# Waiting for all PSUM banks of a dense unit at its head, and for both halves of an expert's up weights at once, in a two-layer flow-matching step

## What the kernel must compute

```python
shift1, scale1, gate1, shift2, scale2, gate2 = adaln(c_vec, w_ada, b_ada)
h = rms_norm(x, norm1) * (1 + scale1) + shift1
conv_in, q_lat, kv_lat, k_rope, gates = split_projection(h @ w_in)
conv_out = conv_module(conv_in, ...)            # GLU, depthwise conv, LayerNorm, swish, @ w_pw2
att = attend(q, k, v) @ w_o                     # 8 heads, latent attention
g_conv, g_att = split(sigmoid(gates))
x = x + gate1 * ((g_conv * conv_out + g_att * att) @ w_out)
h2 = rms_norm(x, norm2) * (1 + scale2) + shift2
# hier_moe: best of 4 groups, best 2 of its 4 experts; 16 experts of width 256
hid = silu(h2 @ w1) * (h2 @ w3) * comb
x = x + gate2 * (hid @ w2)
```

## Time and profile before

| | us |
|---|---|
| three runs | 977.22, 973.48, 974.01 |
| median | 974.01 |
| profiled execution, its own time | 979.21 |
| span of its instructions | 977.4 |
| PE busy with matmuls in the span | 927.7 |
| DVE busy | 726.9 |
| ACT busy | 501.2 |

### The profile page before, as it was taken

One profiled execution on the slowest core, in us unless ns is written; L12 is line 12 of the kernel. 1 busy time (PEld: TensorE's weight loads), 2 busy tenths in 40 slices (PEclk: granted clock), 3 DMA queues, 4 the chain that ended last, 5 costly groups with the idle time before them and its releaser, 6 DMA issues.

```text
span 977.4 us, 15475 instructions
## 1 busy us (share of the span) xinstructions
PE 927.7 (95%) x5998; PEld 770.9 (79%) x5998; DVE 726.9 (74%) x1214; ACT 501.2 (51%) x718; POOL 39.6 (4%) x62
## 2 busy tenths in 40 slices
PE   3999999989999999999999999998899999999997
PEld 2797789767888778887778968996589977888776
DVE  3568799474855689869956697995658568986995
ACT  4243623375422478647754445226663247874772
POOL 1000000032000000000010000001400000000000
PEclk9899999999999799999999999999999999999999
DMA  9953456501655679939939324541123258993971
GB/s 372 369 213 131 168 223 230 201 1 45 231 199 216 254 291 362 361 129 346 385 128 384 113 109 172 232 157 44 44 93 130 81 192 325 361 372 127 326 277 65
DMA packets 29019, 206.75 MB, mean 212 GB/s; under 512 B 3408, under 2 KB 3440, under 8 KB 4240
## 3 DMA queue, kind: packets, MB, share of 16 engines
q1 hardware_dynamic: 28656, 204.81, 55.5%
q0 software_dynamic: 288, 0.92, 0.3%
HBM read 203.98 MB, written 1.74 MB: 210 GB/s over the span
## 4 chain that ended last, share of the span: by engine, by line
PE 80%; DVE 10%; ACT 5%; issue 3%; DMA 1%; DVEq 0%; SPq 0%; ACTq 0%
PE ps L866 57%; PE ps L853 6%; PE ps L877 4%; PE ps L844 2%; PE ps L1331 2%; DVE w_lo L733 2%; PE ps L1154 1%; PE ps L1071 1%; DVE w_lo L728 1%; ACT w_hi L722 1%; DVE x L2359 1%; ACT kT L1611 1%; DMA x<-x 1%; PE ps L1142 1%; PE ps L1426 1%
## 5 line engine op out<-in xcount | busy, mean ns | idle before, releaser
L733 DVE TENSOR_TENSOR w_lo<-ring,w_hi 128x2048 fp32r<-128x2048 f32 (+2 forms) x102 | 225.8, 2222 | 21.6 <-ACT w_hi L1717 20.8
L866 PE MATMUL ps<-h_hi,w_hi 128*128 128x384 f32 x576 | 198.1, 344 | 6.3 <-issue 2.4
L1717 ACT ACTIVATE w_hi<-ring 128x2048 fp32r<-128x2048 f32 x96 | 183.1, 1914 | 20.8 <-PE ps L866 20.8
L866 PE MATMUL ps<-h_hi,w_lo 128*128 128x384 f32 x576 | 193.4, 336 | 0.0
L866 PE MATMUL ps<-h_lo,w_hi 128*128 128x384 f32 x576 | 193.3, 336 | 0.0
L866 PEld LDWEIGHTS ps<-h_hi,w_hi 128*128 128x128 f32 x576 | 108.1, 188 | 20.8 <-issue 13.0
L728 DVE TENSOR_TENSOR w_lo<-ring,w_hi 128x2048 fp32r<-128x2048 f32 x41 | 93.7, 2289 | 33.3 <-ACT w_hi L722 33.3
L866 PEld LDWEIGHTS ps<-h_lo,w_hi 128*128 128x128 f32 x576 | 108.2, 188 | 0.0
L866 PEld LDWEIGHTS ps<-h_hi,w_lo 128*128 128x128 f32 x576 | 108.1, 188 | 0.0
L1961 DVE SCALAR_TENSOR_TENSOR z<-u,par,z 128x399 f32<-128x399 f32 x180 | 104.7, 632 | 1.5
L866 PE MATMUL ps<-w_hi,hg_hi 128*128 128x512 f32 x256 | 103.2, 403 | 0.8 <-DVE hg_lo L733 0.8
(11 more groups left out here) (270 smaller groups left out, 1407.7 us busy)
## 6 DMA issues: line engine op xcount, KB each, us to landing
ring<-wpre SPq DMA_DIRECT2D x96, 1024.0 KB, 6.9
ring<-wmoe SPq DMA_DIRECT2D x96, 1024.0 KB, 6.5
x<-x SPq DMA_DIRECT2D x1, 1536.0 KB, 7.6
x_out<-x SPq DMA_DIRECT2D x4, 384.0 KB, 3.2
par<-par_in POOLq DMA_DIRECT2D x2, 367.5 KB, 7.0
const<-const_in SPq DMA_DIRECT2D x1, 314.0 KB, 3.1
ckv_out<-ckvT POOLq DMA_DIRECT2D x2, 64.0 KB, 5.1
kr_out<-kr POOLq DMA_DIRECT2D x2, 16.0 KB, 5.1
```

Source lines behind the costliest of these rows:

```text
L733: return nc.vector.tensor_tensor(out, whole, leading.bitcast(F32), ALU.subtract)
L866: m = mm(out, a, b, start=(start and i == 0 and j == 0), stop=(stop and i == n - 1 and j == 2))
L1717: af(w_hi[m % MOE_PLACES], slot(moe_slot(l, m)), ACT.Copy).then_inc(split_hi, 1)
```

## The change

It has two parts. First, a new function `begin_all` makes the waits for all banks of a dense unit ahead of its first product: for every bank it looks up the job that had it before, keeps the last of them per evicting engine, and waits for those. GLU units, gate units and `widen` call it at their heads. In `widen` the wait for the convolution's activations (`await_first`) now stands ahead of the bank waits. Second, `up(e, 0)` of experts 1 to 7 waits until unit m + 1, its own second half, is made as well, and `up(e, 1)` no longer waits for weights. Expert 0 keeps its two waits.

```diff
+                def begin_all(name_indices):
+
+                    last = {}
+                    for name, index in name_indices:
+                        j = JOB[(name, index)]
+                        for n, i, b, _ in [e for e in JOBS[:j] if e[2] == JOBS[j][2]][-1:]:
+                            who, k = TAKEN[(n, i)]
+                            last[who] = max(last.get(who, (-1, None)), (k, (n, i)))
+                    for _, e in last.values():
+                        wait_taken(pe, l, *e)
+                    return [ps_of(name, index) for name, index in name_indices]
+
...
                     w = split_unit("glu", c, KD)
-                    for half, name in enumerate(("glu_a", "glu_b")):
-                        out = begin(name, c)
+                    outs = begin_all([("glu_a", c), ("glu_b", c)])
+                    for half, out in enumerate(outs):
                         split_product(out[:, 0:TOK], w(half * P, (half + 1) * P), tokens).then_inc(psum_full, 1)
...
                     w = split_unit("gate", c, KD)
-                    for half in range(2):
-                        out = begin("gate", 2 * c + half)
+                    outs = begin_all([("gate", 2 * c), ("gate", 2 * c + 1)])
+                    for half, out in enumerate(outs):
                         split_product(out[:, 0:TOK], w(half * P, (half + 1) * P), tokens).then_inc(psum_full, 1)
...
                 def widen(name, n, rhs, await_first=None):
                     w = split_unit(name, n, len(rhs))
-                    for c in range(4):
-                        out = begin(name, n * 4 + c)
-                        if c == 0 and await_first is not None:
-                            await_first()
+                    if await_first is not None:
+                        await_first()
+                    outs = begin_all([(name, n * 4 + c) for c in range(4)])
+                    for c, out in enumerate(outs):
                         split_product(out[:, 0:TOK], w(c * P, (c + 1) * P), rhs).then_inc(psum_full, 1)
...
                         at = e // EPG * P
-                        wait_made(pe, mbase, m)
+                        if e == 0:
+                            wait_made(pe, mbase, m)
+                        elif half == 0:
+
+                            wait_made(pe, mbase, m + 1)
                         if e == 0:
```

## The result

The changed kernel takes 1002.72 us, the median of four runs, where the kernel before takes 974.28 beside it (four runs): ratio 1.0284, interval 1.0263 to 1.0304, 28 us slower. The forecast was 19.9 us slower, 993.9, with a range that ended at 999. Run again beside the last experiments, the changed kernel gave 1.0263 (1.0239 to 1.0287), 26.1 us. The direction and the main mechanism were right; 6 to 9 us were missing. The profiled execution took 1003.08, its span is 1001.3 and its mean granted clock 0.971, against 0.985 before.

The account below looks back on a forecast made before the run. PE was taken to bound the kernel, busy 95% of the span. The terms 6.2 + 5.5 + 2 x 2.4 + 3.4 = 19.9 us on the 974.01 median gave 993.9, range 986 to 999.

Parts of the forecast that it names:

- The hold for bank 0 in both layers: Second `w_o` unit: all four products wait for product 0's eviction; idle 7.3 and 8.3 us, costing 6.2 and 5.5.
- 16.5 forecast: The `w_o` part's predicted terms: 6.2 + 5.5 us for the holds and 2 x 2.4 for the clock.
- The free heads: GLU, gate and `w_pw2` units: their bank waits are long met at the head, so cost 0.
- The hold of 2.6 us at expert 1: First round of each layer: up(1, 0) waits for the `w_lo` of unit 3 and starts 2.6 us later.
- cover of 1.6 at down(0): PE already waits 1.59 us for DVE ahead of down(0), time that the delay at expert 1 runs into.
- the experts cost more: Rival: cover at down(0) is lost and the tight expert heads cost 6.8 us, giving 997.3; chance 0.06.
- 6.2 + 5.5 + 3.4: Waits without the clock: `w_o` unit in layer 0, the same in layer 1, and the experts; 15.1 us.
- The loss by the clock behind each `w_o` hold: PE's idle stretch drops the clock to 1.2 GHz; 2.4 us a layer, ends 0 and 3.0.
- saved wait: 36 bank and 28 weight waits leave PE's queue; worth 0 to 3.1 us, taken as 0.
- 2 x 2.4: The clock's term: 2.4 us in each layer for slower matmuls behind the `w_o` unit's idle stretch.
- the experts: Four tight places a layer, at experts 1 and 4, where up(e, 0) waits for its second half: 3.4 us in all.
- Net 0.9: Cost per layer of expert 1's 2.6 us delay in round 0, after 1.76 us of free time at down(0).

Follow-up runs that it names:

- b: The changed kernel with the experts' waits in `up` as before, so only the dense units' part remains: 991.75 us (1.0175).
- c: The kernel before with one wait added, for bank 0 (product 7) at the head of the second `w_o` unit: 993.31 us (1.0184).
- d: The kernel before with `begin_all` in the GLU and gate units alone: 975.93 us (1.0003).
- m: The changed kernel as it is, measured again beside the last experiments: 1000.79 us (1.0263).
- n: The changed kernel with ten thrown-away matmuls filling expert 1's hold in each layer's first round: 995.83 us (1.0204).
- o: The kernel before with the bank 0 wait at the second `w_o` unit's head and expert 1's wait for both halves: 999.98 us (1.0239).
- g: The kernel before, but `up(e, 0)` of experts 2 to 7 waits for both halves: 980.03 us (1.0052).
- h: The kernel before with `turn` 0 moved ahead of the split of unit 5 in ACT's and DVE's written list: 970.39 us (0.9952).
- i: The kernel before with only expert 1 waiting for both halves, its first-round holds filled with ten thrown-away matmuls: 979.23 us (1.0034).
- j: The changed kernel with thrown-away matmuls in both the `w_o` holds and expert 1's first-round holds: 993.26 us (1.0168).
- k: The kernel before, but only expert 4's first product waits for both halves: 975.84 us (1.0009).

## Why the prediction was right and wrong

**Right.** The hold for bank 0 in both layers, its lengths, and that it is the whole of the dense part: 16.5 forecast, 16 to 18 measured (b, c). The free heads (d). The hold of 2.6 us at expert 1 and its cover of 1.6 at down(0), which the list of waits shows used up in the changed kernel and the rival "the experts cost more" denied. The waits of the change all together: 6.2 + 5.5 + 3.4 = 15.1 forecast, +15.2 at full clock for m. The loss by the clock behind each `w_o` hold: 2.4 forecast, 2.4 and 2.6 in the rows; that the middle between two unlike rows was met so closely is in part luck. No saved wait shows, as costed: in d, whose 22 heads make 18 waits fewer, there is nothing to see. The count of 36 saved bank waits was a slip (the written list of jobs gives 17 a layer, 34), and no term hangs on it.

**Wrong: the size of the clock's term.** It was "2 x 2.4", 4.8 us. The low time of m is 32 us above that of before, by the fit 10.4 us; the 25.6 us between the means of m and before split into 15.2 of waits and 10.4 of clock. The step that failed is the one for "the experts", "Net 0.9": I priced the hold of 2.6 us by what it delays and did not ask what it does to the clock, though the part just before had asked it for `w_o`. The row at hand was an idle time of 4.84 us with a fall of the clock; 2.6 us stood between that and none, and it should have had 2.4 us a layer at least as an upper end. With it the high end of the range would have been 999.2 + 4.8 = 1004, and the range would have held. The Trainium skill ("TensorE: Matmul & The Clock Gate", section "HAM oscillation") says that PE is put back to half rate by such a wait and starts its next burst there: the trace agrees for both `w_o` holds, 0.50 in the hold of layer 0 and behind both. The waits in that section of the Trainium skill are of about 3 to 5 us, longer than expert 1's 2.56, for which the runs alone decide: the clock fell there too, in layer 0 before the burst (0.51), in layer 1 only some 1.5 us into it.

**What that leaves.** Behind expert 1's holds the rows show 2.4 us lost in layer 0 (5.24 against 2.86 in n) and 1.3 in layer 1 (837.22 to 841.51, 4.3 us, against 2.99 in n's layer 0 up to the same product), together 3.7. With 5.0 for `w_o` that is 8.7 of the 10.4. Summed over windows of 1 us, the changed kernel's profile has 58 us of low time, 31 of them at the four holds and 27 elsewhere; the profile of before has 29, none of them at these places. So what the changed kernel has more lies at the holds, and 8.7 us over 31 is 0.28 for each microsecond, near the fit's 0.32. The stretches elsewhere, such as the one around window 814 to 815, come no more often with the holds as far as the profiles tell: 21 us in m, 25 in o and 17 in n, 10 to 32 in d, g, h, i, j and k, which have no unfilled hold of these kinds. Against the forecast's 19.9 the rows add 3.7 at expert 1 and 0.2 at `w_o`, 23.8 in all. That is within the interval of the repeat (23.3 to 28.0) and below that of the first runs (25.6 to 29.6); where the last 2 to 5 us lie is not shown.

## What to carry to other kernels

Merging the waits of one unit at its head was free here where every wait had long been met, and cost the whole distance between the first and the last product where one bank or one half is late: look for that one before adding any such head. Price every new idle stretch of PE twice, by what it delays and by the matmuls behind it at half clock, and do so for the short ones too. A wait that serves as cover for another edit is a loss by itself: moving one entry in the written list of ACT and DVE took four such waits out and made the kernel 4.7 us faster than before.

## What the hardware showed unexpectedly

An idle stretch of 2.56 us, behind 12 matmuls of 5 columns, was enough for the granted clock to fall to 0.51, and the next 12 matmuls of 512 columns started every 0.43 us instead of 0.23. In the kernel before, the idle stretch of 1.59 us ahead of down(0) in the same round left it at 1.00 (windows 353 to 356). What share the near-empty matmuls have in the fall was not tested. Thrown-away matmuls in the hold kept it at 1.00 with the same start of the next product, and took 5 us off the changed kernel in expert 1's two holds and 4 to 8 in `w_o`'s two.

A microsecond at the lower clock cost 0.32 us of the kernel's time over 68 executions of the kernel before, by the fit, and not the 0.5 that a stretch of matmuls at half speed would. At the holds the reason is in the rows: part of the low time lies in the hold itself, where PE waits anyway. For the stretches of the kernel before it was not looked for. The kernel's spread from run to run, 973 to 980 us, goes for the most part with this low time.
